# The z projection cut into 16 parts between the attention units, with the tiles around it in another order

## The chip, the core and the metric

The kernel runs on one core of a Trainium2 chip. The metric is the device time of one launch in microseconds (us); lower is better. The core has five engines that run side by side and meet at semaphores: TensorE (PE), VectorE (DVE), ScalarE (ACT), GpSimd (POOL) and SyncE (SP), which issues most of the transfers.

## What is computed

One layer of a hybrid backbone for 128 context tokens and 512 latent tokens (640 in all), width 1024, everything in f32:

```python
x += 0.5*gate1*SwiGLU1(mod(RMSNorm(x)))
h  = mod(RMSNorm(x))
q,k,v (conv, DeltaNet) | z | decay,beta | q_b,k_b,v_b (attention) = h @ w_in
o_a = rmsnorm(delta_forward + delta_backward) * silu(z)      # 8 heads of 64
o_b = rmsnorm(softmax_1 @ v_b - lam * softmax_2 @ v_b)       # 4 heads of 128
x += gate2 * (concat(o_a, o_b) @ w_out)
x += 0.5*gate3*SwiGLU2(mod(RMSNorm(x)))
```

z has 512 columns and is not read before the gate of the DeltaNet output, late in the layer. q_b and k_b also have 512 columns each; they are rotated and then used by the attention.

## The kernel before

Activations lie transposed, features on the partitions and the 640 tokens along the row. A projection goes by **tiles** of 128 output columns: its weights (128x1024) arrive in `w_raw`, ACT rounds them to `w_hi`, DVE makes the rest `w_lo`, and PE runs `dense` (line 1740): for each of 8 blocks of input features and each half of 320 tokens three matmuls (`product`: hi*lo, lo*hi, hi*hi), 48 in all. Two buffers of weights alternate. Every engine's instructions stand in an order written out by hand, and an engine that waits at a semaphore holds up all that stands behind it.

The mixer goes through these stages:

- **Projections.** PE does the 4 z tiles first (ACT applies Silu as it copies them from PSUM into `z_t`), then 12 tiles of q, k and v with the short convolution on DVE, then a loop `for m in range(12, 28)`. It has the last conv tiles (m 12 to 15), q_b (16 to 19), k_b (20 to 23) and v_b (24 to 27, `values`). Within it run a norm of q and k (the helpers of line 2058 and `l2_scale`) and, from m = 20, eight rotations (`rotate`, one a step).
- **Attention units.** `ATT_UNITS` lists 20 units: 4 of the context (128 keys) and 16 of 128 latent queries against 640 keys. In step v PE does `scores(v + 1)` (line 2089, 64 rows deep), `weigh(v - 2)` (line 2110) and `turn(v - 1)` (line 2099, transposes); DVE does the maxima, the combination of the two softmax maps and the copy out; ACT the exponentials and the copy of the turned weights. After every fourth unit comes a **norm** in four steps k (squares on PE, line 2137; root on ACT; spread on PE, line 2123; product on DVE, line 1423), started at v = 6, 10, 14, 18, 22. It has PSUM bank 7, the units' result bank 6. Its result goes to `h_hi[1]`, `h_lo[1]`, which until then hold half of the mixer's input h.
- **Delta tiles**, a list made by `make_schedule` on PE, DVE and POOL, which ends with the first scan step.
- **Scan steps** s = 1 to 4, each with `scan_a`, `scan_b`, `scan_c` on PE for four chains b, and `scan_r`, `scan_u`, `scan_out` on DVE. Between the stages PE does an `attention_part`, 12 matmuls of the attention's half of `w_out`; 16 parts make 8 column blocks m, and DVE adds each to x (`update_attention(m)`).
- **Output.** The DeltaNet output is normed (`o_mean`, `o_norm`), turned (`turn_out`), gated with z (`o_gate`), split (`o_low`, three of five on POOL, line 1726) and multiplied by its half of `w_out`: blocks m = 0 to 3 whole, then `PARTS[2] = [6, 7, 4, 5]` in halves of tokens. The weights of blocks 2i and 2i+1 come as one tile; the last two arrive at places `OUT_POS` 7 and 10 of the ring. FFN 2 follows.

## Time and profile before

| | |
|---|---|
| median of 3 runs | 1712.5 us (1708.83 to 1721.85) |
| the profiled execution | 1717.91 us, span 1715.9 us |
| PE busy | 1642.2 us (96%) |
| weight load busy | 1542.0 us (90%) |
| DVE, ACT, POOL busy | 949.5, 512.2, 208.3 us |
| mean granted clock of TensorE | 0.974 |

The span runs from the first to the last instruction; 2 us of the device time lie around it. Times of places below are us from its start. The clock of TensorE is given as a share of 2.4 GHz; it has two levels, 1.00 and 0.50. A matmul's end is modelled and overlaps the next one's start, so how fast PE really goes is read from the starts. A 32-bit matmul appears as two records, so 4 matmuls of scores are shown as x8.

### The profile page before, as it was taken

Reading aid. Unit: us, or ns where it says so; the run is one execution under the profiler, and the core shown is the slowest. Engines: PE = TensorE matmul, PEld = TensorE weight load, DVE = VectorE, ACT = ScalarE, POOL = GpSimd, SP = SyncE. Lnnn points to the kernel's source line nnn. Section 1 sums busy time; section 2 is a strip of 40 time slices with the busy share of each in tenths; the row PEclk is TensorE's granted clock in tenths of the full one; section 3 lists DMA queues with packets and bytes.
Section 4 is the critical chain, followed back from the end, with each engine's and each line's share of the span. In section 5 each row is a group of like instructions: output and inputs, shape, how many; then the busy total and the mean of one; then the engine's idle time right before and its main releaser. Section 6 shows DMA issues by size and latency. Waiting matters only on the chain.

```text
span 1715.9 us, 27316 instructions
## 1 busy us (share of the span) xinstructions
PE 1642.2 (96%) x10807; PEld 1542.0 (90%) x10807; DVE 949.5 (55%) x1767; ACT 512.2 (30%) x978; POOL 208.3 (12%) x168
## 2 busy tenths in 40 slices
PE   5999999999999999998989999999899999999998
PEld 4899999999999999985778888898899999998886
DVE  5866776666365575436846787676652223321233
ACT  4522222221214434424541111263442222222223
POOL 0000000000000000120015666665000000000000
PEclk9899999999999999996988999998999999999999
DMA  9444444444244122210000000002112222223222
GB/s 279 124 129 147 138 133 136 144 147 147 86 138 132 52 74 73 60 53 13 1 7 1 1 1 1 19 26 74 38 48 75 73 73 73 73 61 98 68 79 87
DMA packets 183811, 136.53 MB, mean 80 GB/s; under 512 B 8192, under 2 KB 169269, under 8 KB 183605
## 3 DMA queue, kind: packets, MB, share of 16 engines
q1 hardware_dynamic: 161029, 112.91, 22.0%
q10 hardware_dynamic: 22704, 22.55, 4.3%
q8 instruction: 53, 0.87, 0.2%
q14 instruction: 25, 0.20, 0.0%
HBM read 132.03 MB, written 3.41 MB: 79 GB/s over the span
## 4 chain that ended last, share of the span: by engine, by line
PE 84%; DVE 9%; issue 2%; ACT 2%; SPq 2%; DMA 1%; POOL 0%; DVEq 0%; ACTq 0%; POOLq 0%
PE ps L1736 19%; PE ps L1737 18%; PE ps L1738 18%; PE ps L2283 3%; PE ps L1883 3%; PE ps L1882 3%; PE ps L1881 3%; PE ps L2287 3%; PE ps L2089 2%; PE ps L1792 1%; PE ps L2211 1%; SPq L434 1%; PE ps L2110 1%; PE ps L2290 1%; PE ps L2263 1%
## 5 line engine op out<-in xcount | busy, mean ns | idle before, releaser
L1736 PE MATMUL ps<-h_hi,w_lo 128*128 128x320 f32 x1760 | 554.2, 315 | 10.8 <-DVE w_lo L1010 4.1
L1737 PE MATMUL ps<-h_lo,w_hi 128*128 128x320 f32 x1760 | 546.9, 311 | 0.0
L1738 PE MATMUL ps<-h_hi,w_hi 128*128 128x320 f32 x1760 | 546.9, 311 | 0.0
L1010 DVE TENSOR_TENSOR w_lo<-w_raw,w_hi 128x1024 fp32r<-128x1024 f32 x158 | 196.0, 1242 | 369.7 <-ACT w_hi L563 368.7
L1736 PEld LDWEIGHTS ps<-h_hi,w_lo 128*128 128x128 f32 x1760 | 333.6, 190 | 15.2 <-DVE h_lo L1056 5.3
L1737 PEld LDWEIGHTS ps<-h_lo,w_hi 128*128 128x128 f32 x1760 | 333.6, 190 | 1.1 <-issue 0.7
L1738 PEld LDWEIGHTS ps<-h_hi,w_hi 128*128 128x128 f32 x1760 | 333.3, 189 | 0.0
L563 ACT CAST w_hi<-w_raw 128x1024 fp32r<-128x1024 f32 x158 | 165.2, 1047 | 215.6 <-PE ps L1738 110.7
L1143 DVE SCALAR_TENSOR_TENSOR ada_acc<-ada_ffn,cond,ada_acc 128x256 f32<-128x256 f32 x336 | 139.0, 479 | 1.1
L657 ACT CAST act_hi<-scratch 128x640 f32 (+1 forms) x44 | 32.0, 728 | 292.1 <-DVE scratch L1183 292.1
L1736 PE MATMUL ps<-act_hi,w_lo 128*128 128x320 f32 (+1 forms) x352 | 109.5, 311 | 0.0
L1738 PE MATMUL ps<-act_hi,w_hi 128*128 128x320 f32 (+1 forms) x352 | 108.7, 309 | 0.0
L1737 PE MATMUL ps<-act_lo,w_hi 128*128 128x320 f32 (+1 forms) x352 | 108.7, 309 | 0.0
L1881 PE MATMUL ps<-w_hi,act_lo 128*128 128x512 f32 x220 | 87.0, 395 | 1.1 <-DVE w_lo L1010 1.1
L1883 PE MATMUL ps<-w_hi,act_hi 128*128 128x512 f32 x220 | 87.5, 398 | 0.0
L1882 PE MATMUL ps<-w_lo,act_hi 128*128 128x512 f32 x220 | 86.9, 395 | 0.0
L1183 DVE TENSOR_TENSOR scratch<-square,ps 128x640 f32<-128x640 f32 x44 | 36.1, 821 | 87.4 <-PE ps L1738 87.4
L650 ACT ACTIVATE square<-ps 128x640 f32<-128x640 f32 x44 | 31.0, 705 | 170.9 <-PE ps L1738 170.6
L1643 POOL MEMSET pre<- 128x24 f32 x3 | 0.2, 121 | 548.7 <-PE ps L1738 548.7
L1737 PEld LDWEIGHTS ps<-act_lo,w_hi 128*128 128x128 f32 x352 | 66.2, 188 | 0.1
L1736 PEld LDWEIGHTS ps<-act_hi,w_lo 128*128 128x128 f32 x352 | 66.2, 188 | 0.1
L1738 PEld LDWEIGHTS ps<-act_hi,w_hi 128*128 128x128 f32 x352 | 66.2, 188 | 0.0
(322 smaller groups left out, 2499.8 us busy)
## 6 DMA issues: line engine op xcount, KB each, us to landing
w_raw<-in_w_ffn_in SPq DMA_DIRECT2D x84, 512.0 KB, 3.8
w_raw<-in_w_ffn_out SPq DMA_DIRECT2D x44, 512.0 KB, 3.8
ada_ffn<-in_w_ada ACTq DMA_DIRECT2D x43, 512.0 KB, 3.6
w_raw<-in_w_in SPq DMA_DIRECT2D x28, 512.0 KB, 3.8
ada_ffn<-in_w_ada SPq DMA_DIRECT2D x13, 512.0 KB, 4.5
ada_tile<-in_w_ada SPq DMA_DIRECT2D x10, 512.0 KB, 8.7
w_raw<-in_w_out SPq DMA_DIRECT2D x8, 512.0 KB, 3.4
ada_wide<-in_w_ada SPq DMA_DIRECT2D x3, 1024.0 KB, 9.7
```

The costliest lines, as they stand in the source:

```text
L563: nc.scalar.copy(w_hi[s if slot is None else slot], w_raw[s][:]).then_inc(w_hi_ready, 1)
L1010: nc.vector.tensor_tensor(w_lo[at], w_raw[s][:], w_hi[at].bitcast(F32), ALU.subtract)\
L1143: ins = nc.vector.scalar_tensor_tensor(a, w, col, a, op0=ALU.mult, op1=ALU.add)
L1183: nc.vector.tensor_tensor(halves(act_f[par][:]), halves(silu_g[par][:]), ps[:, 4 * par + 2:4 * par + 4, 0:HT], ALU.mult).then_inc(act_read ...
L1736: nc.tensor.matmul(out, lo, xh, start=start, stop=False)
L1737: nc.tensor.matmul(out, hi, xl, start=False, stop=False)
L1738: return nc.tensor.matmul(out, hi, xh, start=False, stop=stop)
L1881: nc.tensor.matmul(out, lo, wh, start=first, stop=False)
L1882: nc.tensor.matmul(out, hi, wl, start=False, stop=False)
L1883: ins = nc.tensor.matmul(out, hi, wh, start=False, stop=last)
L2283: four(c, lambda out, h: nc.tensor.matmul(out, m_t[c][:, h, :], t_cols[c][:, h, :], start=True, stop=True))
L2287: four(c, lambda out, h: nc.tensor.matmul(out, x_w[c][:, h, :], tt_cols[c][:, h, :], start=True, stop=True))
```

## The change

- **Projections.** The z tiles no longer come first. The 4 q_b tiles take their place, copied to `q_b`. The loop runs over `m in range(12, 32)`: k_b goes in half tiles (24 matmuls a step, m 16 to 23) and v_b in half tiles (m 24 to 31). The steps of the q and k norm and the rotations keep their numbers m, so they lie closer together.
- **z in the attention.** `z_part(c)`, c = 0 to 15, does 12 matmuls (4 input blocks, one half of the tokens) into bank 6. Steps v = 0 to 2 have two parts, v = 3 to 12 one. Each second part ends a group, and ACT copies it to `z_t` (`z_evict`); the next group waits for that copy. Weights of the z tiles are split in between by ACT and DVE. Silu of z is applied in place later on ACT, between the first `scan_kg` and `scan_first`, with two loads of the activation tables.
- **Norms** start at v = 13, 15, 17, 19, 22 and use bank 6; the units' results go to bank 7.
- **Last scan step.** On PE an attention part stands after each of its stages; before it stood only after the last. On DVE `scan_u` goes ahead of `update_attention(4)` and `o_mean`; `o_norm` of the last three tiles stands ahead of the gates. Three parts are left for the output stage, after `turn_out(2)`, `(3)` and `(4)`; before there were five.
- **w_out.** The tile of blocks 6 and 7 is loaded at place 7 and that of 4 and 5 at place 10; before the two stood the other way round, while the products were done in the order 6, 7, 4, 5.

```diff
@@ -36,7 +36,10 @@
 NU = len(ATT_UNITS)
-NORM_END = NU + 6
+NORM_START = [13, 15, 17, 19, 22]
+NORM_END = NORM_START[-1] + 4
+Z_PARTS = [2, 2, 2, 1, 1, 1, 1, 1, 1, 1, 1, 1, 1]
+Z_DONE = [n for n in range(len(Z_PARTS)) for c in range(sum(Z_PARTS[:n]), sum(Z_PARTS[:n + 1])) if c % 2 == 1]
...
@@ -86,9 +89,9 @@
-def norm_at(v):
-    return divmod(v - 6, 4) if v >= 6 else (None, None)
+def norm_at(v, k):
+    return NORM_START.index(v - k) if v - k in NORM_START else None
...
@@ -122,13 +125,14 @@
 TILE_WIN = FFN_TILES
-TILE_WBV = TILE_WIN + 24
+TILE_WBV = TILE_WIN + 20
+TILE_Z = TILE_WIN + 24
 TILE_WOUT = TILE_WIN + 28
...
 OUT_POS, FFN_EARLY = [0, 1, 2, 3, 4, 5, 7, 10], [6, 8, 9, 11]
-OUT_RING = [0, 1, 2, 3, 4, 5, 6, 7]
+OUT_RING, OUT_COLS = [0, 1, 2, 3, 4, 5, 6, 7], [0, 1, 2, 3, 0, 1, 3, 2]
 TILE_LAST = TILE_FFN[0] + N_IN + 11
@@ -750,7 +757,7 @@
                 act.wait_ge(tile_done, TILE_WIN + i + 1)
-                nc.scalar.activation(halves(z_t[:, i, :]), ps[:, 2 * i:2 * i + 2, 0:HT], ACT.Silu).then_inc(proj_out, 1)
+                nc.scalar.copy(halves(q_b[:, i, :]), ps[:, 2 * i:2 * i + 2, 0:HT]).then_inc(proj_out, 1)
             act.wait_ge(pads_set, 3)
...
@@ -760,11 +767,11 @@
             act.wait_ge(mix_in, 16 * 11)
-            for m in range(12, 28):
+            for m in range(12, 32):
                 if m < 16:
                     to_conv(m - 4, m % 2)
-                elif m < 27:
-                    w_high(TILE_WIN + m + 1, (m + 1) % 2)
+                elif m % 2 == 0:
+                    w_high(TILE_WIN + m // 2 + 9, (m // 2 + 9) % 2)
                 if m < 17:
...
@@ -818,6 +825,11 @@
             ins.then_inc(vb_ready, 1)
+            w_high(TILE_Z + 1, 1)
+            def z_evict(g):
+                act.wait_ge(z_mm, g + 1)
+                nc.scalar.copy(half_of(z_t[:, g // 2, :], g % 2), ps[:, 6, 0:HT]).then_inc(z_out, 1)
...
@@ -851,18 +863,26 @@
                     weights_out(v - 2)
-                j, k = norm_at(v)
-                if k == 0:
+                for g in range(2 * HB):
+                    if Z_DONE[g] == v:
+                        z_evict(g)
+                if v in (2, 5):
+                    i = 2 if v == 2 else 3
+                    w_high(TILE_Z + i, i % 2)
+                j = norm_at(v, 3)
+                if j is not None:
+                    act.wait_ge(an_tmp, j + 1)
+                    nc.scalar.copy(heads4_of(h_hi[1], j), heads4(scratch[0][:, 0:512], P)).then_inc(an_hi, 1)
+                j = norm_at(v, 1)
+                if j is not None:
+                    act.wait_ge(an_mm, j + 1)
+                    nc.scalar.activation(tok_rs[:, 0:4], ps[:, 6, 0:4], ACT.Ln, bias=eps_col[:], scale=D / P).then_inc(an_log, 1)
+                    act.wait_ge(an_log, j + 1)
+                    nc.scalar.activation(tok_rs[:, 0:4], tok_rs[:, 0:4], ACT.Exp, scale=-0.5).then_inc(an_rs, 1)
+                j = norm_at(v, 0)
+                if j is not None:
                     act.wait_ge(s_out, 4 * j + 4)
                     nc.scalar.activation(heads4(square[0][:, 0:512], P), heads4_of(att_q, j), ACT.Square).then_inc(an_sq, 1)
-                if k == 1:
-                    act.wait_ge(an_mm, j + 1)
-                    nc.scalar.activation(tok_rs[:, 0:4], ps[:, 7, 0:4], ACT.Ln, bias=eps_col[:], scale=D / P).then_inc(an_log, 1)
-                    act.wait_ge(an_log, j + 1)
-                    nc.scalar.activation(tok_rs[:, 0:4], tok_rs[:, 0:4], ACT.Exp, scale=-0.5).then_inc(an_rs, 1)
-                if k == 3:
-                    act.wait_ge(an_tmp, j + 1)
-                    nc.scalar.copy(heads4_of(h_hi[1], j), heads4(scratch[0][:, 0:512], P)).then_inc(an_hi, 1)
...
@@ -928,6 +948,9 @@
                 scan_kg(0, b)
+            for i in range(HB):
+                nc.scalar.activation(z_t[:, i, :], z_t[:, i, :], ACT.Silu)
+            load_power_table()
             for b in range(4):
...
@@ -1416,16 +1439,21 @@
                     att_out(v - 2)
-                if k == 2:
+                if v in (3, 6):
+                    i = 2 if v == 3 else 3
+                    w_low(TILE_Z + i, i % 2)
+                j = norm_at(v, 3)
+                if j is not None:
+                    dve.wait_ge(an_hi, j + 1)
+                    nc.vector.tensor_tensor(heads4_of(h_lo[1], j), heads4(scratch[0][:, 0:512], P),
+                                            heads4_of(h_hi[1], j).bitcast(F32), ALU.subtract).then_inc(an_done, 1)
+                j = norm_at(v, 2)
+                if j is not None:
                     dve.wait_ge(an_spread, j + 1)
...
                     nc.vector.scalar_tensor_tensor(heads4(scratch[0][:, 0:512], P), heads4_of(att_q, j), dn_col[:],
-                                                   heads4(ps[:, 7, :], P), op0=ALU.mult, op1=ALU.mult).then_inc(an_tmp, 1)
-                if k == 3:
-                    dve.wait_ge(an_hi, j + 1)
-                    nc.vector.tensor_tensor(heads4_of(h_lo[1], j), heads4(scratch[0][:, 0:512], P),
-                                            heads4_of(h_hi[1], j).bitcast(F32), ALU.subtract).then_inc(an_done, 1)
+                                                   heads4(ps[:, 6, :], P), op0=ALU.mult, op1=ALU.mult).then_inc(an_tmp, 1)
...
@@ -1563,12 +1591,12 @@
                     update_attention(0)
+                for b in range(4):
+                    scan_u(s, b)
                 if s == NT - 1:
...
                         o_mean(p)
-                for b in range(4):
-                    scan_u(s, b)
                 if s == 1:
...
@@ -1586,11 +1614,10 @@
                 o_mean(p)
-            o_norm(2)
+            for p in range(2, NT):
+                o_norm(p)
             o_gate(0)
             o_gate(1)
-            for p in range(OUT_EARLY, NT):
-                o_norm(p)
             update_attention(5)
...
@@ -2033,15 +2061,21 @@
-            for m in range(12, 28):
-                pe.wait_ge(w_lo_ready, TILE_WIN + m + 1)
+            for m in range(12, 32):
+                tile = m if m < 16 else m // 2 + 8
+                pe.wait_ge(w_lo_ready, TILE_WIN + tile + 1)
                 if m < 24:
-                    pe.wait_ge(proj_out, m - 1)
-                    dense(m % 2, 2 * (m % 2)).then_inc(tile_done, 1)
+                    pe.wait_ge(proj_out, tile - 1)
+                    if m < 16:
+                        dense(m % 2, 2 * (m % 2)).then_inc(tile_done, 1)
+                    elif m % 2 == 0:
+                        dense(tile % 2, 2 * (tile % 2), only=0)
+                    else:
+                        dense(tile % 2, 2 * (tile % 2), only=1).then_inc(tile_done, 1)
                 else:
                     if m == 24:
-                        pe.wait_ge(proj_out, 24)
-                    values(m - 24)
+                        pe.wait_ge(proj_out, 20)
+                    values(m // 2 - 12, m % 2)
                 if m == 13:
...
@@ -2107,42 +2141,66 @@
                     vals = cv_tok[:, hb * P:(hb + 1) * P] if nk > P and kt == 0 else v_b[:, kt, hb * P:(hb + 1) * P]
-                    ins = nc.tensor.matmul(ps[:, 6, 0:P], vals, att_wt[:, kt * P:(kt + 1) * P],
+                    ins = nc.tensor.matmul(ps[:, 7, 0:P], vals, att_wt[:, kt * P:(kt + 1) * P],
                                            start=(kt == 0), stop=(kt == nk // P - 1))
...
             pe.wait_ge(vb_ready, 1)
+            def z_part(c):
+                i, half, q = c // 4, c // 2 % 2, c % 2
+                if c % 4 == 0:
+                    pe.wait_ge(w_lo_ready, TILE_Z + i + 1)
+                if c % 2 == 0 and c >= 2:
+                    pe.wait_ge(z_out, c // 2)
+                for k in range(4 * q, 4 * q + 4):
+                    w = (w_hi[i % 2][:, k * P:(k + 1) * P], w_lo[i % 2][:, k * P:(k + 1) * P])
+                    x = [half_of(h[k // 4][:, k % 4, :], half) for h in (h_hi, h_lo)]
+                    ins = product(ps[:, 6, 0:HT], k, w, x, k == 0, k == KD - 1)
+                    if (half, k) == (1, 5):
+                        ins.then_inc(tile_done, 1)
+                if q == 1:
+                    ins.then_inc(z_mm, 1)
             scores(0)
+            z_parts = iter(range(4 * HB))
             for v in range(NORM_END):
-                j, k = norm_at(v)
-                if k == 2:
+                j = norm_at(v, 2)
+                if j is not None:
                     pe.wait_ge(an_rs, j + 1)
                     for i in range(4):
-                        ins = nc.tensor.matmul(ps[:, 7, i * P:(i + 1) * P], tok_rs[:, i:i + 1].broadcast_to([P, P]), ident[:],
+                        ins = nc.tensor.matmul(ps[:, 6, i * P:(i + 1) * P], tok_rs[:, i:i + 1].broadcast_to([P, P]), ident[:],
                                                start=True, stop=True)
                     ins.then_inc(an_spread, 1)
+                if v < len(Z_PARTS):
+                    z_part(next(z_parts))
                 if v + 1 < NU:
...
                     weigh(v - 2)
+                if v < len(Z_PARTS) and Z_PARTS[v] == 2:
+                    z_part(next(z_parts))
                 if 1 <= v <= NU:
                     turn(v - 1)
-                if k == 0:
+                j = norm_at(v, 0)
+                if j is not None:
                     pe.wait_ge(an_sq, j + 1)
...
                     for i in range(4):
-                        ins = nc.tensor.matmul(ps[:, 7, i:i + 1], square[0][:, i * P:(i + 1) * P], ones_d[:, 0:1],
+                        ins = nc.tensor.matmul(ps[:, 6, i:i + 1], square[0][:, i * P:(i + 1) * P], ones_d[:, 0:1],
                                                start=True, stop=True)
...
             for i in range(2 * NT):
+                if i == 2:
+                    pe.wait_ge(an_tmp, 5)
                 if i == 3:
-                    pe.wait_ge(an_tmp, 5)
+                    pe.wait_ge(s_out, NU)
                 if i >= 4:
...
@@ -2295,9 +2353,8 @@
                         stage(s, b)
-                    if (s, stage) != (3, scan_a) and (s < NT - 1 or stage is scan_c):
+                    if (s, stage) != (3, scan_a):
                         attention_part(next(parts))
-            attention_part(next(parts))
...
@@ -2313,13 +2370,12 @@
             turn_out(1)
-            attention_part(next(parts))
             turn_out(2)
-            attention_part(next(parts))
             attention_part(next(parts))
...
             turn_out(4)
+            attention_part(next(parts))
             pe.wait_ge(o_lo, NT)
...
@@ -2328,7 +2384,7 @@
                 for n, m in enumerate(PARTS[2]):
-                    i = 4 + m // 2
+                    i = 9 - m // 2
                     pe.wait_ge(w_lo_ready, TILE_WOUT + OUT_POS[i] + 1)
...
```

How the engines' orders differ at three places. First PE in the steady part of the attention: a step before is scores, weigh (two rows), turn, and then the next scores.

```order
2404 L2089 MATMUL ps<-k_all,q_b 128x320 x4
2405 L2110 MATMUL ps<-att_wt,cv_tok 128x128
2406 L2110 MATMUL ps<-att_wt,v_b 128x128 x4
2407 L2099 MATMUL ps<-ident,sumsq 128x128 x5
2408 L2089 MATMUL ps<-k_all,q_b 128x320 x4
```

The same place on PE in the changed kernel, where lines 1763 to 1765 are `product`.

```order
2349 L1765 MATMUL ps<-h_hi,w_hi 128x320
2350 L2123 MATMUL ps<-k_all,q_b 128x320 x4
2351 L2144 MATMUL ps<-att_wt,cv_tok 128x128
2352 L2144 MATMUL ps<-att_wt,v_b 128x128 x4
2353 L2133 MATMUL ps<-ident,sumsq 128x128 x5
2354 L1763 MATMUL ps<-h_hi,w_lo 128x320
2355 L1764 MATMUL ps<-h_lo,w_hi 128x320
```

Twelve matmuls of a z part now stand between one step's turn and the next step's scores.

Second, PE in the last scan step, before: `scan_a` (2182), `scan_b` (2197) and `scan_c` (2211) one behind the other, then a part.

```order
2830 L2182 MATMUL ps<-st,pre 128x128 x16
2831 L2197 MATMUL ps<-r_s,m_t 128x64 x4
2832 L2197 MATMUL ps<-r_s,x_w 128x64 x4
2833 L2197 MATMUL ps<-r_s,t_cols 128x64 x4
2834 L2197 MATMUL ps<-r_s,tt_cols 128x64 x4
2835 L2211 MATMUL ps<-r_s,m_t 128x64 x4
```

In the changed kernel, PE in the same step (2255 is `scan_b`):

```order
2844 L1765 MATMUL ps<-h_hi,w_hi 128x320
2845 L2255 MATMUL ps<-r_s,m_t 128x64 x4
2846 L2255 MATMUL ps<-r_s,x_w 128x64 x4
2847 L2255 MATMUL ps<-r_s,t_cols 128x64 x4
2848 L2255 MATMUL ps<-r_s,tt_cols 128x64 x4
2849 L1763 MATMUL ps<-h_hi,w_lo 128x320
2850 L1764 MATMUL ps<-h_lo,w_hi 128x320
```

A part of 12 matmuls stands on either side of `scan_b`.

Third, DVE in that step, before: the update of x (three rows), `o_mean`, and only then `scan_u` (1452).

```order
889 L1061 SCALAR_TENSOR_TENSOR x_t<-ps,mods,x_t 128x128
890 L1061 SCALAR_TENSOR_TENSOR x_t<-ps,mods,x_t 128x192
891 L1061 SCALAR_TENSOR_TENSOR x_t<-ps,mods,x_t 128x320
892 L1535 TENSOR_REDUCE o_sum<-t_all 128x8 x3
893 L1452 TENSOR_TENSOR r_s<-ps,beta 128x256 x4
```

DVE there in the changed kernel:

```order
890 L1480 TENSOR_TENSOR r_s<-ps,beta 128x256 x4
891 L1084 SCALAR_TENSOR_TENSOR x_t<-ps,mods,x_t 128x128
892 L1084 SCALAR_TENSOR_TENSOR x_t<-ps,mods,x_t 128x192
893 L1084 SCALAR_TENSOR_TENSOR x_t<-ps,mods,x_t 128x320
894 L1563 TENSOR_REDUCE o_sum<-t_all 128x8 x3
```

`scan_u` now stands ahead of both.

## Rows read from the trace of the kernel before

**Rows 1.** Page, busy time of each engine.

```profile
PE 1642.2 (96%) x10807; PEld 1542.0 (90%) x10807; DVE 949.5 (55%) x1767; ACT 512.2 (30%) x978; POOL 208.3 (12%) x168
```

**Rows 2.** Stretches: length, PE, PEld, DVE, ACT, POOL busy (x), PEclk, DMA share, GB/s.

```profile
732.00:741.00 9.00, 9.00 (x56) 8.20 (x55) 4.36 (x4) 3.10 (x5) 2.15 (x1) 1.00 0.21 58
...
784.00:806.00 22.00, 21.63 (x58) 13.76 (x58) 14.14 (x36) 8.29 (x22) 0.00 (x0) 0.50 0.00 1
806.00:865.00 59.00, 56.84 (x337) 42.34 (x335) 48.84 (x116) 32.88 (x85) 0.00 (x0) 1.00 0.00 1
...
850.00:860.00 10.00, 9.75 (x53) 6.66 (x52) 8.89 (x22) 5.24 (x13) 0.00 (x0) 1.00 0.00 0
```

**Rows 3.** Timeline of PE, first matmuls of two successive tiles (start, us, instruction).

```profile
578.68 0.31 PE L1736 MATMUL ps<-h_hi,w_lo 128*128 128x320 f32 x1
...
585.72 0.31 PE L1736 MATMUL ps<-h_hi,w_lo 128*128 128x320 f32 x1
```

**Rows 4.** Timeline of PE from projection to context units, and ACT's copy between.

```profile
772.27 0.40 PE L2005 MATMUL ps<-w_hi,h_hi 128*128 128x512 f32 x1
...
775.39 0.69 PE L2086 MATMUL ps<-k_b,q_b 64*128 64x128 f32 x4 [1.87 <-ACT v_b L819]
...
772.70 2.54 ACT L819 COPY v_b<-ps 128x512 f32<-128x512 f32 x5 [6.26 <-PE ps L2005]
```

**Rows 5.** Timeline of PE, scores and turn in latent units.

```profile
807.42 1.35 PE L2089 MATMUL ps<-k_all,q_b 64*128 64x320 f32 x8
...
816.61 2.25 PE L2089 MATMUL ps<-k_all,q_b 64*128 64x320 f32 x8
...
820.64 1.34 PE L2089 MATMUL ps<-k_all,q_b 64*128 64x320 f32 x4
...
859.58 2.77 PE L2089 MATMUL ps<-k_all,q_b 64*128 64x320 f32 x8
```

**Rows 6.** Groups of DVE's norm operations in the attention (busy us, mean ns, idle).

```profile
L1423 DVE SCALAR_TENSOR_TENSOR scratch<-q_b,dn_col,ps 128x512 f32<-128x512 f32 x5 | 3.7, 741 | 3.3 <-PE ps L2123 3.3
L1427 DVE TENSOR_TENSOR h_lo<-scratch,h_hi 128x512 fp32r<-128x512 f32 x4 | 2.7, 681 | 0.0
```

**Rows 7.** Timeline of PE, norm steps and the end of the attention.

```profile
849.40 1.06 PE L2123 MATMUL ps<-ident,tok_rs 128*128 128x128 f32 x8
...
864.04 0.95 PE L2137 MATMUL ps<-ones_d,square 128*128 128x1 f32 x8
...
878.62 1.70 PE L2149 MATMUL ps<-ident,pre 128*128 128x128 f32 x7
```

**Rows 8.** Stretches behind the scans, columns as in group 2.

```profile
1175.00:1183.00 8.00, 8.00 (x37) 8.00 (x37) 3.28 (x8) 0.90 (x2) 2.07 (x3) 0.50 0.20 51
...
1199.00:1204.00 5.00, 4.97 (x24) 4.97 (x25) 4.44 (x8) 1.14 (x2) 0.00 (x0) 0.68 0.35 105
...
1220.00:1232.00 12.00, 12.00 (x74) 11.84 (x73) 4.39 (x12) 2.01 (x5) 0.00 (x0) 0.89 0.27 79
```

**Rows 9.** Timeline of ACT around the first scan step, and an earlier table load.

```profile
1061.73 3.92 ACT L897 ACTIVATE square<-k_tok,ekg 128x64 f32<-128x64 f32 x16
1090.29 0.53 ACT L907 COPY st<-ps 64x128 f32<-64x128 f32 x2 [24.64 <-PE ps L2211]
...
681.57 1.28 ACT L773 ACT_TABLE_LOAD   x1
```

**Rows 10.** Timeline of PE and POOL, last scan step to the output's matmuls.

```profile
1174.65 1.76 PE L2211 MATMUL ps<-r_s,m_t 128*128 128x64 f32 x8 [1.13 <-DVE r_s L1452]
...
1181.29 0.61 PE L1736 MATMUL ps<-h_hi,w_lo 128*128 128x320 f32 x1
...
1199.03 0.64 PE L1736 MATMUL ps<-h_hi,w_lo 128*128 128x320 f32 x1 [2.22 <-DVE h_lo L1556]
...
1188.76 3.37 POOL L1726 TENSOR_TENSOR h_lo<-scratch,h_hi 128x512 fp32r<-128x512 f32 x2 [11.69 <-ACT h_hi L966]
```

**Rows 11.** Waits of PE from 1210 to 1222 (total, times, longest).

```profile
PE ps L1736 <- DVE w_lo L1010: 3.3, 1, 3.3
```

44 lines of the change are left out of this document (24 added, 20 removed).

## Prediction

> **What bounds the kernel now.** I read the page first, then PE in stretches, then the timelines at the places that the change touches. PE is busy 96% of the span [rows 1], so a gain must come from PE's idle time or from time in which it is slow; the change takes no matmul away. A busy share hides both. In the attention PE shows 56.84 of 59 us busy at a clock of 1.00, and 21.63 of 22 us at 0.50 [rows 2]. The reader should see two things. First, from 784 to 806 every matmul takes twice its time. Second, at full clock eleven steps (807.42 to 859.58) take 52.2 us, 4.74 each with their norms, while one step in which PE never waited took 4.03 (816.61 to 820.64, its scores 2.25 instead of 2.77) [rows 5]. In a stretch of two steps without norms DVE is busy 8.89 of 10 us [rows 2], 4.1 us of a 4.6 us step. DVE and the chain through it set the pace there, and PE has about 0.6 us of slack a step. Elsewhere PE waits and is slow at three places behind the scans [rows 8, 10, 11].
>
> The Trainium skill (Trainium Kernel Development and Optimization, "Performance Expectations") says that a matmul's busy time is a bad measure and that the busy share of weight loads is a good one. By the former the attention has 2 us of room, by the latter (42.34 of 59 us, rows 2) some 17 us; the starts bear out the latter.
>
> **1. The projections lose four tiles.** A tile of 48 matmuls takes 7.04 us (578.68 to 585.72) [rows 3], 1.76 per 12. Four tiles: -28.2 us. k_b and v_b in half tiles cost PE nothing, since its weight loads are per matmul anyway. What runs beside them gets closer: a step of the loop has 3.5 us of projection instead of 7.0. A step with norm and rotation took 9 us with DVE busy 4.36, ACT 3.10 and POOL 2.15 [rows 2]; it becomes 5.4 us long (9 less half a tile of 3.5), which still covers each of them, and w_hi and w_lo are made in every second step only. So I take 0 (bounds 0 and +2, for waits in the chain of that norm). The copy of v_b that PE waits for stays: 2.54 us, with scores starting 3.1 us after the last values matmul started [rows 4].
>
> **2. The attention takes the z parts.** Before, from the first scores at 775.39 to the turns of k at 878.62: 103.2 us [rows 4, 7]. After, at full clock:
> - Steps 0 to 2: six parts, 10.6 us; the small context matmuls, some 0.7 a step, 2.1; three waits for the eviction of bank 6. A copy of 512 columns takes 0.5 us (a fifth of 2.54 [rows 4]), with the signals 0.6 each, 1.8. Together 14.5.
> - Steps 3 to 5: three parts 5.3, three scores of 2.2, the rest 1.6: 13.5.
> - Steps 6 to 12: a full step and a part, 4.03 + 1.76 = 5.79 on PE against DVE's 4.1. Seven: 40.5. PE becomes the bound, and DVE's chain has 1.7 us more to answer in.
> - Steps 13 to 18: no z, but a norm every second step. On PE 0.9 for squares and 1.0 for the spread [rows 7] make 5.0 a step; on DVE 0.74 + 0.68 [rows 6] make 4.8. The squares of norm j now wait for the product of norm j-1 in the same step, and DVE does that product behind the copy of the weighed unit: about 0.3 a step more. Six times 5.1 to 5.3: 31.
> - Steps 19 to 25: before, 864.95 (end of the squares) to 878.62, 13.7 us; one norm more falls into it: 15.
>
> Sum 114.5, against 103.2: +11.3 for 28.2 us of work, net -16.9. To this comes the clock. The 3.1 us without matmuls before the first scores will bring it to 0.50, as it did at 776. The question is how long. Before, it stayed at 0.50 until 806 under scores 64 rows deep, PE busy all the time [rows 2]. With dense projection matmuls it came back in 3 to 5 us: from 1199 the mean is 0.68 over 5 us of them, so some 3.2 us were slow, and from 1220 it is 0.89 over 12 us, 2.6 us slow [rows 8]. After the change dense parts follow at once, so I take 4 us at half speed, +2 (bounds 0 and the rival below). For signals between a part and its neighbours 0.15 to 0.2 in some 13 steps, +2.5. **Net -12.4** (bounds -17 and -3).
>
> **3. Silu of z** goes to ACT behind `scan_kg`, where ACT is idle 24.64 us [rows 9]: four Silus of 640 columns at some 0.75 and two loads at 1.28 [rows 9] make 5.6. Cost 0; without that cover it would be on the scan's chain. The Trainium skill (ScalarE: Activation LUTs, "What ACT_TABLE_LOAD costs") puts a switch at about 2.66 us with its drain. By that it would be 8.3 us, still hidden; no row here shows the drain.
>
> **4. The last scan step.** DVE's update and `o_mean` make PE wait 1.13 us before `scan_c`, after which the clock is 0.50 from 1175 to 1183 [rows 8, 10]. `scan_c` takes 6.6 us there (1174.65 to 1181.29) against 3.5 at full clock. After, `scan_b` ends with `scan_u` right behind it and a part on PE in between: no wait, and no fall of the clock. Before, PE had done a and b when it began to wait, at 1173.5 (1174.65 less 1.13). Two parts of 1.8 now lie among them, so `scan_c` starts at 1177.1 and ends at 1180.6 instead of 1181.3. Behind it stands one part instead of two, and at full speed: the first turn comes at 1182.4 instead of some 1186. From the first turn: two gates 1.4 and the norms before them bring the first split to 1187.4, against 1188.7 before; POOL then has three, at 1.7 each (3.37 for two) to 2.2 when DVE runs beside it [rows 10]: 1192.5 to 1194. The update of block 5, on which a part waits, adds idle PE time, not length. The output's matmuls start at 1194.2 instead of 1199.03, **-4.8** (bounds -8 and -1). PE will idle longer here than before, so the low clock at their start stays.
>
> **5. The w_out tiles.** PE waits 3.3 us for the last tile's `w_lo` [rows 11]. After, blocks 6 and 7 (3.5 us of halves) come first, and the late tile is needed 3.5 us later, when it is just ready. The stretch after the wait has a mean clock of 0.89 over 12 us [rows 8], 1.3 us lost, which goes too. **-4.5** (bounds -5 and -1, if the new order of blocks waits for an update of x instead).
>
> Delta tiles and scans 1 to 3 do the same as before: 0.
>
> **Sum**: -12.4 - 4.8 - 4.5 = -21.7. The profiled execution took 1717.9 us, so 1696.2 by itself; it lies 5.4 above the median of 1712.5, and the forecast for the median is **1691 us**.
>
> **The rivals.**
> - *The attention is bound by latency, not by PE.* Then a z part adds to a step of 4.6 instead of filling its slack: 6.4 for seven steps (+4), 5.7 for the six with norms (+2.5), and one us more in the last ones. For it: the maxima wait for scores and scores for exponentials in turn, and a part stands ahead of the scores. Against: the one unhindered step, and that the exponentials of the step before can run under the part. Total -14: **1698**. The same time comes out if terms 4 and 5 only move their waits on.
> - *The low clock lasts (slower).* The place is the start of the attention. If the scores' 64 rows keep the clock at 0.50 as they did for 30 us before, the z parts pay double too: 28 us of full-speed work in steps 0 to 5 take 56, +28 instead of +2. That turns the gain into +4, and each further step costs 5.8: with the first two heavy steps, **1728**. It decides when the slow stretch holds more than 24 us of full-speed work. Before, that stretch had long runs of scores alone; now at most 2.2 us stand between two parts. That speaks against it.
> - *The clock is back at once and the output's chain shrinks by the full 8 us.* Then -12.4 becomes -15, term 4 -7.5, and the sum is -27: **1685**.
>
> **How the numbers follow.** Forecast (1686 to 1696) 0.5; latency or moved waits 0.27; better case 0.15; slow clock 0.06; nothing of it works 0.02. The range of 8 in 10 takes in the first three but for their outer ends: 1681 to 1703. A measurement of this kernel tells a difference of about 1%, 17 us, from none. Below 1695.4 lie most of the forecast's own range and the better case: faster 0.61. Slower by 1% needs the slow clock: 0.05. Same 0.34.
>
> **What would show it.** In the profile after: first scores near 747 to 748; the granted clock back at 1.00 by some 753; steps 6 to 12 at 5.8 to 6.0 us; turns of k near 866; no wait of `scan_c` for `r_s` and a clock of 1.00 there; the output's matmuls 4 to 5 us closer to the end of the scan; no wait for `w_lo` behind block 3. The prediction is wrong if steps with z take 6.4 us or more, if the clock is 0.50 past step 3, or if the projections gain less than 27 us because the norm of q and k or a rotation holds PE up.

## Result and the profile after

| | before | changed |
|---|---|---|
| median | 1714.61 us (1708.83 to 1721.85, 4 runs) | 1691.34 us (1687.52 to 1693.84, 4 runs) |
| ratio, 95% interval | | 0.9851, [0.981, 0.9892] |
| profiled execution, span | 1717.91, 1715.9 us | 1687.52, 1685.7 us |
| mean granted clock | 0.974 | 0.991 |

The change takes 1.5% away; by the interval it is 1.1 to 1.9%, all of it beyond the 1% that the prediction took for the least that can be told. The two profiled executions lie 30.4 us apart and the medians 23.3: the one of before is 3.3 above its median, the other 3.8 below. So a difference between the two traces, taken stage by stage, overstates the gain by some 7 us in all.

The page of the changed kernel:

```profile
PE 1612.6 (96%) x10807; PEld 1518.5 (90%) x10807; DVE 945.2 (56%) x1767; ACT 518.0 (31%) x988; POOL 207.1 (12%) x168
```

Against [rows 1] the number of PE's records is the same and the busy share is the same 96%. That line alone says nothing of where 30 us went. The starts of five instructions do. Each is read from the timeline of its own kernel; e1, e2, e3 and r1 are runs told of below, r1 a second run of the changed kernel.

| start, us | before | changed | e1 | e2 | e3 | r1 |
|---|---|---|---|---|---|---|
| first scores | 775.39 | 748.40 | 775.41 | 774.15 | 747.97 | 748.84 |
| turns of k | 878.62 | 865.78 | 877.86 | 887.88 | 865.41 | 871.39 |
| last `scan_a` | 1166.27 | 1149.00 | 1160.30 | 1171.22 | 1148.52 | 1153.82 |
| output's matmuls | 1199.03 | 1175.75 | 1191.38 | 1197.99 | 1176.48 | 1180.57 |
| FFN 2 | 1235.41 | 1205.67 | 1222.83 | 1232.93 | 1211.45 | 1210.47 |
| span | 1715.9 | 1685.7 | 1703.8 | 1713.2 | 1692.0 | 1693.4 |

From before to changed: projections -27.0, attention +14.1 (103.2 to 117.4), turns of k to the last `scan_a` -4.4, to the output's matmuls -6.0, to FFN 2 -6.5, the rest -0.4: -30.2.

The attention of before is not one number, though. e1 and e2 have the same instructions there as before, and it took 103.2 us in before, 102.5 in e1 and 113.7 in e2; the changed kernel's took 117.4, 117.4 (e3) and 122.6 us (r1). The +14.1 is one pair out of these; the means of three and three differ by 12.7. The clock goes with it. The attention of before, changed and e2 as stretches (columns as in [rows 2]; each line is of the kernel whose starts it has):

```profile
775.39:878.62 103.23, 94.53 (x476) 69.48 (x477) 72.61 (x188) 49.15 (x135) 0.00 (x0) 0.83 0.02 6
748.40:865.78 117.38, 106.33 (x668) 86.76 (x669) 75.83 (x191) 54.63 (x146) 0.00 (x0) 0.97 0.06 19
774.15:887.88 113.73, 99.85 (x477) 75.24 (x478) 72.85 (x188) 49.57 (x135) 0.00 (x0) 0.77 0.02 5
```

**The attention.** Timeline of PE in the changed kernel: the first scores, three steps with a z part, and steps with a norm (lines 1763 to 1765 are `product`, 2123 scores, 2144 weigh, 2133 turn, 2193 squares, 2207 turns of k). A part's first matmul is shown; its other eleven are in the dots:

```profile
748.40 0.49 PE L2120 MATMUL ps<-k_b,q_b 64*128 64x128 f32 x4 [2.73 <-ACT v_b L826]
...
801.92 2.01 PE L2123 MATMUL ps<-k_all,q_b 64*128 64x320 f32 x8
...
805.54 0.39 PE L1763 MATMUL ps<-h_hi,w_lo 128*128 128x320 f32 x1
...
807.48 1.84 PE L2123 MATMUL ps<-k_all,q_b 64*128 64x320 f32 x8
809.25 0.49 PE L2144 MATMUL ps<-att_wt,cv_tok 128*128 128x128 f32 x2
809.57 1.06 PE L2144 MATMUL ps<-att_wt,v_b 128*128 128x128 f32 x8
810.47 0.71 PE L2133 MATMUL ps<-ident,sumsq 128*128 128x128 f32 x5
810.93 0.39 PE L1763 MATMUL ps<-h_hi,w_lo 128*128 128x320 f32 x1
...
812.87 2.01 PE L2123 MATMUL ps<-k_all,q_b 64*128 64x320 f32 x8
...
822.85 1.35 PE L2123 MATMUL ps<-k_all,q_b 64*128 64x320 f32 x8
...
832.97 1.02 PE L2193 MATMUL ps<-ones_d,square 128*128 128x1 f32 x8 [0.86 <-DVE scratch L1455]
...
844.43 1.02 PE L2193 MATMUL ps<-ones_d,square 128*128 128x1 f32 x8 [1.24 <-DVE scratch L1455]
...
865.78 6.62 PE L2207 MATMUL ps<-ident,pre 128*128 128x128 f32 x40
```

The reader should compare the scores. Between 801.92 and 812.87 steps follow each other by 5.56 and 5.39 us; the six from the scores at 780.01 to those at 812.87 take 32.9, 5.48 each, where 5.79 was forecast. The eight records span 2.01 and 1.84 us there, but 1.35 at 822.85, as at 807.42 in [rows 5]. So a step's own work on PE is 1.94 (the part, 805.54 to 807.48) + 1.29 (from the scores at 822.85 to the weigh behind them) + 1.22 + 0.46 (809.25 to 809.57 to 810.47 to 810.93) = 4.91, and 0.57 of the 5.48 is still a wait of scores, inside a group that shows no wait: at 801.92 the second map's first matmul starts 0.67 us after the first map's, at 822.85 it starts 0.01 after.

The waits of PE from 745 to 870 (total, times, longest):

```profile
PE ps L2120 <- ACT v_b L826: 2.7, 1, 2.7
PE ps L2193 <- DVE scratch L1455: 2.7, 3, 1.2
PE ps L2123 <- ACT exps L858: 2.3, 3, 0.9
PE ps L2193 <- ACT square L885: 2.2, 1, 2.2
...
PE ps L1763 <- ACT z_t L832: 1.4, 3, 0.5
```

The second line is new: squares of one norm wait for the product of the norm before. Stretches of the changed kernel (columns as in [rows 2]):

```profile
748.00:760.00 12.00, 10.58 (x70) 9.36 (x71) 5.27 (x21) 4.42 (x17) 0.00 (x0) 1.00 0.16 45
775.00:822.00 47.00, 46.02 (x285) 37.02 (x283) 34.90 (x84) 24.05 (x60) 0.00 (x0) 1.00 0.08 23
822.00:852.00 30.00, 25.61 (x165) 20.02 (x163) 21.23 (x50) 16.07 (x43) 0.00 (x0) 0.94 0.00 1
878.00:920.00 42.00, 34.34 (x249) 30.30 (x248) 26.60 (x54) 7.16 (x23) 27.11 (x22) 0.92 0.00 1
1149.00:1176.00 27.00, 24.32 (x191) 23.60 (x190) 21.88 (x41) 14.02 (x39) 14.04 (x12) 1.00 0.22 63
```

In 775:822 PE is busy 98% at a clock of 1.00; in 822:852, where z is done and the norms stand, 85% at 0.94. The last line is the last scan step, at full clock throughout; before it had 0.50 from 1175 to 1183 [rows 8]. 878:920 is the start of the delta tiles, whose instructions are the same in both kernels, and still the clock differs there, since the same stretch before shows 0.72:

```profile
878.00:920.00 42.00, 35.25 (x201) 31.01 (x199) 18.40 (x44) 13.84 (x37) 17.29 (x14) 0.72 0.03 7
```

**Silu.** Timeline of ACT in the changed kernel:

```profile
1044.47 3.92 ACT L917 ACTIVATE square<-k_tok,ekg 128x64 f32<-128x64 f32 x16
1048.40 1.28 ACT L952 ACT_TABLE_LOAD   x1
1049.70 2.62 ACT L952 ACTIVATE z_t<-z_t 128x640 f32<-128x640 f32 x4
1052.32 1.28 ACT L599 ACT_TABLE_LOAD   x1
...
1073.03 0.53 ACT L927 COPY st<-ps 64x128 f32<-64x128 f32 x2 [19.42 <-PE ps L2269]
```

It takes 5.2 us (1048.40 to 1053.60), and ACT then waits 19.42 us for PE: hidden, as forecast.

**The output.** Timeline of PE in the changed kernel:

```profile
1175.75 0.42 PE L1763 MATMUL ps<-h_hi,w_lo 128*128 128x320 f32 x1 [1.05 <-DVE h_lo L1584]
```

Neither `scan_c`'s wait for `r_s` nor the 3.3 us for `w_lo` is there any more. PE waits 1.05 us before the output's matmuls where it waited 2.22 [rows 10]; "PE will idle longer here than before" was wrong. The clock behind this wait, in the changed kernel and then in e3, which waits 2.22 us there:

```profile
1175.00:1180.00 5.00, 4.25 (x29) 4.25 (x30) 4.83 (x10) 1.79 (x2) 0.00 (x0) 1.00 0.34 111
1176.00:1181.00 5.00, 4.52 (x20) 4.52 (x21) 4.75 (x9) 1.60 (x2) 0.00 (x0) 0.66 0.33 105
```

All three profiles with the wait of 2.2 us have the low clock behind it (0.68 in before, 0.66 in e1 and e3), none of the eleven with 1.05 to 1.08 us has it.

### The profile page after: what moved, and what is told of

The parts are those of the page before. It is cut to its first block, busy times and chain, and to the rows that moved or that the text cites. A ratio compares the mean times of both kernels' runs of the same rounds, so it can differ in the third digit from the quotient of the medians.

```text
span 1685.7 us, 27313 instructions
## 1 busy us (share of the span) xinstructions
PE 1612.6 (96%) x10807; PEld 1518.5 (90%) x10807; DVE 945.2 (56%) x1767; ACT 518.0 (31%) x988; POOL 207.1 (12%) x168
## 4 chain that ended last, share of the span: by engine, by line
PE 85%; DVE 9%; ACT 2%; SPq 2%; issue 2%; DMA 1%; POOL 0%; DVEq 0%; ACTq 0%; POOLq 0%
PE ps L1763 19%; PE ps L1765 19%; PE ps L1764 19%; PE ps L2341 3%; PE ps L1910 3%; PE ps L1909 3%; PE ps L1908 3%; PE ps L2345 3%; PE ps L1819 1%; PE ps L2123 1%; PE ps L2255 1%; PE ps L2269 1%; SPq L439 1%; PE ps L2348 1%; PE ps L2144 1%
```

## Experiments

The kernel before ran beside each; ratios are against it, with the 95% interval. A ratio is not always the quotient of the two medians (for e1 that is 0.9939), and medians of runs that were not measured together are compared with care: before has 1714.6, 1721.7, 1717.6 and 1716.8 us beside changed, e1 to e4, e5 to e8, and the rest. Four groups: parts of the change alone, the amount and place of z's work, the two waits that the change made, and repeats.

**e1_tiles_only**: the kernel before with the order of the last two w_out tiles alone.

```diff
-OUT_RING = [0, 1, 2, 3, 4, 5, 6, 7]
+OUT_RING, OUT_COLS = [0, 1, 2, 3, 4, 5, 6, 7], [0, 1, 2, 3, 0, 1, 3, 2]
...
-                    i = 4 + m // 2
+                    i = 9 - m // 2
```

Expected:

> The kernel before with one change: the weight tile of output blocks 6 and 7 arrives at place 7 of the ring and that of 4 and 5 at place 10. My account (term 5): the 3.3 us wait of PE for w_lo goes, and with it the low clock behind it, 4 to 6 us less than before (ratio 0.997). Rival, that the wait only moves to an update of x or to the late tile: within 1 us of before.

Measured: 1711.16 us (1704.82 to 1717.37), ratio 0.9964 [0.9938, 0.9991]. The wait for `w_lo` is gone. From the output's matmuls to FFN 2 it takes 31.45 us instead of 36.38, -4.9. The medians differ by more (1721.7 of before in these runs), but the interval holds -1.5 to -10.7 us and so says no more than the trace does. This is what was expected, and not the rival's 1 us.

**e2_scan_only**: the kernel before with the last scan step and the output stage reordered, as in the changed kernel.

```diff
+                for b in range(4):
+                    scan_u(s, b)
                 if s == NT - 1:
                     update_attention(4)
                     for p in range(OUT_EARLY):
                         o_mean(p)
-                for b in range(4):
-                    scan_u(s, b)
...
-                    if (s, stage) != (3, scan_a) and (s < NT - 1 or stage is scan_c):
+                    if (s, stage) != (3, scan_a):
```

Expected:

> The kernel before with the last scan step and the output stage of the changed one: scan_u ahead of the update of x and of the sums, a part after each stage on PE, norms ahead of the gates. My account (term 4): no wait before scan_c, no fall of the clock there, the output's matmuls 5 to 6 us closer to the start of the step; 5 to 6 us less. Rival, that the late tile of weights then holds PE up longer, since the ring did not get faster: only 1 to 3 us less, and the wait for w_lo grows from 3.3 us.

Measured: 1715.4 us (1705.24 to 1717.09), ratio 0.9959 [0.9935, 0.9984]. Last `scan_a` to the output's matmuls: 26.77 us instead of 32.76, 6.0 closer, where 5 to 6 were expected. The wait for `w_lo` stays at 3.3 us and doesn't grow, against the rival. The stretch of it, in e2:

```profile
1171.00:1198.00 27.00, 24.30 (x192) 23.57 (x190) 21.77 (x40) 13.81 (x39) 14.28 (x12) 1.00 0.24 67
```

The clock stays at 1.00. The waits of PE from 1150 to 1222 in e2 begin with the one that this part doesn't touch:

```profile
PE ps L1735 <- DVE w_lo L1010: 3.3, 1, 3.3
PE ps L1735 <- DVE h_lo L1556: 1.1, 1, 1.1
```

**e3_z_only**: the changed kernel with both of these as before.

```diff
-                    i = 9 - m // 2
+                    i = 4 + m // 2
...
-                for b in range(4):
-                    scan_u(s, b)
                 if s == NT - 1:
                     update_attention(4)
                     for p in range(OUT_EARLY):
                         o_mean(p)
+                for b in range(4):
+                    scan_u(s, b)
```

Expected:

> The changed kernel with the last scan step, the output stage and the w_out tiles as before, so the z parts, the half tiles and the late norms alone. My account: 12 to 13 us less than before up to the turns of k, and the same gain at the end, ratio 0.9925. Rival, that the gain of the z parts is lost again behind them: under 8 us. If the delta tiles gain 4 us more, as in the profile of the changed kernel, that is the clock and not the change, and the ratio comes out between 0.990 and 0.993.

Measured: 1697.72 us (1693.78 to 1705.93), ratio 0.988 [0.9844, 0.9916]. The waits of PE from 1150 to 1222 in e3:

```profile
PE ps L1764 <- DVE w_lo L1033: 3.3, 1, 3.3
PE ps L1764 <- DVE h_lo L1584: 2.2, 1, 2.2
...
PE ps L2270 <- DVE r_s L1480: 1.1, 1, 1.1
```

The old waits are back, `w_lo`, `h_lo` (L1584) and `r_s` alike. Yet last `scan_a` to the output's matmuls takes 27.96 us here and not 32.76: after the same 1.1 us of waiting the clock did not fall this time (1.00 over 1148 to 1177, where e1 has 0.89 over 1160 to 1192). With the old order the stretch takes 32.76 (before), 31.08 (e1) and 27.96 us (e3); with the new one it takes 26.75 to 26.77 in all eleven profiles that have it (e2, changed, e4 to e9, r1 to r3). So the reorder itself is worth 27.96 - 26.75 = 1.2, and beside that it takes away a loss to the clock that was 3.1 and 4.8 us in two profiles of three and none in the third. z alone gives 1.2% (0.8 to 1.6%, 14 to 27 us), and the 0.9925 that was expected lies outside the interval: the z parts bring more than the account had for them. e1 and e2 give 0.4% each by their ratios, too little to be told apart by times. The three ratios add up to 2.0% against the 1.5% of the whole, which their intervals allow.

**e4_third_z**: the changed kernel with 4 of the 12 matmuls of each part.

```diff
-                    ins = product(ps[:, 6, 0:HT], k, w, x, k == 0, k == KD - 1)
+                    ins = nc.tensor.matmul(ps[:, 6, 0:HT], w[0], x[0], start=(k == 0), stop=(k == KD - 1))
```

Expected:

> The changed kernel with only the hi*hi product in the z parts, so 4 of 12 matmuls each; z then lacks its two correction products. 128 matmuls of 0.147 us, 18.8 us, leave PE. If PE bounds the steps with z, they shrink by nearly all of it, 14 to 18 us in the attention. If the parts lie in slack of the chain of maxima and exponentials, steps 6 to 12 cannot go below 4.6 us: they lose 0.8 of 1.18 us each, and the whole attention 9 to 12 us.

Measured: 1689.05 us (1685.33 to 1696.26), ratio 0.9813 [0.977, 0.9857]; 2 us below the changed kernel by the medians, 0.4% by the ratios, whose intervals overlap, for 18.8 us of matmuls less (two thirds of 28.2). Its profiled execution is the longest of the four, and its attention takes 125.6 us, more than the 117.4 with all of z. Both expectations missed. Stretches of e4:

```profile
748.00:760.00 12.00, 9.95 (x40) 7.49 (x41) 5.69 (x24) 4.86 (x18) 0.00 (x0) 0.63 0.17 45
767.00:850.00 83.00, 74.14 (x350) 57.03 (x348) 52.90 (x125) 37.52 (x94) 0.00 (x0) 0.77 0.06 20
```

And its waits of PE from 749 to 875:

```profile
PE ps L2123 <- ACT exps L858: 6.1, 7, 1.4
PE ps L2193 <- DVE scratch L1455: 5.3, 3, 2.7
```

The changed kernel has a clock of 0.98 in 767:850 and the kernel before 0.81. With a third of z the scores wait seven times for exponentials, and the clock averages 0.77. So it can't say what a step would take at full clock with less work. What it points to is another use of the parts: with them whole, PE stays at its higher level. The stretches are of one profile, but the mean clock of whole executions agrees: 0.977 to 0.984 in the four of e4, 0.987 to 0.991 in the four of the changed kernel.

**e5_late_parts**: no part in steps 0 to 2, two each in steps 3 to 8.

```diff
-Z_PARTS = [2, 2, 2, 1, 1, 1, 1, 1, 1, 1, 1, 1, 1]
+Z_PARTS = [0, 0, 0, 2, 2, 2, 2, 2, 2, 1, 1, 1, 1]
...
```

Expected:

> The changed kernel with no z part in steps 0 to 2 and two in each of steps 3 to 8 (weight splits moved along). My account: the dense parts in the context steps fill waits and keep the clock up. Without them PE waits 2 to 4 us in steps 0 to 2 and the clock falls to 0.50 there until the parts of step 3, so 4 to 8 us more than the changed kernel. Rival, that the context steps' waits cost nothing because the same matmuls only move: within 1.5 us.

Measured: 1696.39 us (1691.33 to 1698.87), ratio 0.9871 [0.9839, 0.9903]; attention 121.7 us. The context units wait for exponentials three times, 2.4 us in all, and the clock from 748 to 760 is 0.57:

```profile
748.00:760.00 12.00, 9.56 (x35) 7.54 (x36) 7.14 (x30) 4.18 (x19) 0.00 (x0) 0.57 0.18 46
```

A mean of 0.57 of two levels puts (1 - 0.57) / 0.5 = 86% of the 12 us at half speed. Behind them, under parts two a step, it is 1.00 (767 to 850). It comes back in the first part of step 3, of which the first and the last matmul in e5 are:

```profile
755.69 0.61 PE L1763 MATMUL ps<-h_hi,w_lo 128*128 128x320 f32 x1
...
758.77 0.45 PE L1765 MATMUL ps<-h_hi,w_hi 128*128 128x320 f32 x1
```

Its matmuls stand 0.27 us apart, at half speed, and those of the next part 0.15. So the low clock lasted 10 us here and 24 to 31 with the order of before (before, e1, e2), which has no dense matmuls at this place. The time itself tells little: the attention is 4.3 us longer than the changed kernel's 117.4, as expected, but shorter than the 122.6 that the same changed kernel took in r1.

**e6_product_first**: on DVE the norm's product goes to the head of its step, ahead of the maxima.

```diff
             for v in range(NORM_END):
+                j = norm_at(v, 2)
+                if j is not None:
+                    dve.wait_ge(an_spread, j + 1)
...
                 if v + 1 < NU:
                     att_max(v + 1, 0)
```

Expected:

> The changed kernel with the product of a norm at the head of DVE's step instead of its end. The squares then do not wait for it: PE's three waits for that product, 2.7 us in sum, go, and the fall of the clock at 846 with them: 2.5 to 5 us less than the changed kernel in the attention. Rival, that the steps with norms are bound by DVE's sum of work (4.8 us a step), so that the wait moves to the scores: under 1 us.

Measured: 1687.31 us (1683.56 to 1691.86), ratio 0.9828 [0.9797, 0.9859]. The wait of the squares is gone; in e6 they follow the turn at once:

```profile
830.86 0.71 PE L2133 MATMUL ps<-ident,sumsq 128*128 128x128 f32 x5
831.40 0.95 PE L2193 MATMUL ps<-ones_d,square 128*128 128x1 f32 x8
832.28 1.90 PE L2123 MATMUL ps<-k_all,q_b 64*128 64x320 f32 x8
```

Its attention takes 113.0 us against 117.4, both with a clock of 1.00 in 748:760: -4.3, within the 2.5 to 5 that were expected. Of it 2.7 are the waits for the product; squares also wait 1.0 us for ACT instead of 2.2, and scores 1.6 for exponentials instead of 2.3. The clock hardly has a part in it: at half speed are 6.0 us of the changed kernel's attention and 5.4 of this one's, 0.3 us of loss apart, and the fall at 846 that was to go is there in e6 at 845.

**e8_part_ahead**: the first z part goes ahead of PE's wait for `v_b`.

```diff
-            pe.wait_ge(vb_ready, 1)
...
+            z_part(next(z_parts))
+            pe.wait_ge(vb_ready, 1)
             scores(0)
```

Expected:

> The changed kernel with z part 0 ahead of the first scores, in the 2.7 us in which PE waits for the copy of v_b. Part of 1.76 us moves into the wait: 1.5 to 1.8 us less than the changed kernel. Rival, that the context steps are a chain through the evictions, in which the part was hidden already: under 0.5 us.

Measured: 1690.54 us (1685.73 to 1693.55), ratio 0.9843 [0.9813, 0.9874]. PE's wait there falls from 2.73 to 0.88 us, and the attention, from first scores to turns of k, from 117.4 to 116.8. The turns of k come 1.5 us earlier (864.31), but 0.9 of this is there at the first scores already (747.52 instead of 748.40), and without this edit they start anywhere from 747.53 to 748.84. So 0.6 us is what the trace gives to the edit, less than the 1.5 to 1.8 expected: the part went into the gap, and a new wait of 1.1 us for the exponentials stands behind the first scores. The median moves by less than can be told.

**e7_both**: e6 and e8 together.

```diff
+            z_part(next(z_parts))
+            pe.wait_ge(vb_ready, 1)
             scores(0)
...
+                j = norm_at(v, 2)
+                if j is not None:
+                    dve.wait_ge(an_spread, j + 1)
```

Expected:

> The changed kernel with both edits, the norm's product at the head of DVE's step and z part 0 ahead of the first scores. The gains are at different places and should add: 4 to 6.5 us less than the changed kernel. If either is hidden, the sum of what the two single runs show.

Measured: 1685.88 us (1683.78 to 1690.21), ratio 0.9809 [0.9779, 0.9839]. Beside it e6 has 1687.31 us, so what e8's edit adds can't be told here either. Against the changed kernel's 1691.34 it is 5.5 us less, as expected, but the two weren't measured together.

**Repeats**, measured together on one chip: the changed kernel, e7 and e6 again.

Expected:

> The changed kernel once more, on the chip of the next three. Ratio to before 0.985 as in its first four runs, 0.981 to 0.989. Its profile tells how far the low clock moves between runs of one kernel: the step from the turns of k to the second scan step took 231.7 us after 236.1 before with the same instructions, which I put down to 6.8 against 20.5 us at half clock there.

> The changed kernel with the norm's product at the head of DVE's step and z part 0 ahead of the first scores, beside the changed kernel on the same chip: 4 to 6 us less if the single runs add (4.3 us in the attention of the first, 0.6 of the second in the profiles); within 2 us of it if the clock eats it.

> The changed kernel with only the norm's product at the head of DVE's step, beside the changed kernel on the same chip: 3 to 5 us less, and again no wait of the squares for the product.

Measured, six runs each: r1 1692.1 us (1688.7 to 1695.17), 0.9846 [0.9811, 0.9882]; r2 1684.99 us (1684.45 to 1698.7), 0.9828 [0.9787, 0.987]; r3 1685.73 us (1681.73 to 1689.17), 0.9809 [0.9773, 0.9844]. The product first is 6.4 us better than the change as it is (3 to 5 were expected), the second time that it comes out lower; both together are 7.1 better (4 to 6), so the part ahead adds nothing that can be told. The clock of r1 at the start of the attention:

```profile
748.00:760.00 12.00, 10.64 (x53) 9.32 (x54) 4.21 (x17) 3.57 (x12) 0.00 (x0) 0.72 0.16 45
```

It is the same kernel with the same wait for `v_b`, and here 0.72 instead of 1.00: 56% of 12 us at half speed, 3.4 us lost, in an attention of 122.6 us.

**e9_part_between**: in steps 6 to 12 the z part stands between the scores of the two softmax maps.

```diff
                 for m in range(2):
+                    if m == 1 and between is not None:
+                        between()
```

Expected:

> The changed kernel with the z part of steps 6 to 12 between the scores of the two maps instead of ahead of both. The trace shows 8 records of scores in 1.35 us where nothing waits and 4 in 1.34 us where the second map waits, so the matmuls of the two maps, on rows 0 to 63 and 64 to 127, seem to run side by side. If so, the part parts them and a step costs some 0.5 to 1.0 us more, 4 to 7 us over the seven. Rival, that the second map's wait for its exponentials is what makes the scores long: the part then fills that wait, and the steps get shorter, by up to 0.3 us each.

Measured: 1702.49 us (1698.06 to 1707.02), ratio 0.9916 [0.9882, 0.9949]: 10.4 us more than r1 by the medians; its attention takes 129.3 us against r1's 122.6, both with a clock of 0.72 in 748:760. These 6.7 us are within the 4 to 7 expected and are what the traces place; the other 3.7 of the medians they do not. Timeline of PE in e9:

```profile
790.78 1.34 PE L2125 MATMUL ps<-k_all,q_b 64*128 64x320 f32 x4
792.05 0.49 PE L2146 MATMUL ps<-att_wt,cv_tok 128*128 128x128 f32 x2
792.38 1.06 PE L2146 MATMUL ps<-att_wt,v_b 128*128 128x128 f32 x8
793.27 0.71 PE L2135 MATMUL ps<-ident,sumsq 128*128 128x128 f32 x5
793.91 1.34 PE L2125 MATMUL ps<-k_all,q_b 64*128 64x320 f32 x4
795.18 0.41 PE L1763 MATMUL ps<-h_hi,w_lo 128*128 128x320 f32 x1
```

None of these scores waits, and one map alone (x4) takes 1.34 us: as long as both together where nothing parts them (x8, 1.35 at 822.85 of the changed kernel, where their starts are 0.01 us apart). The two maps have their 64 rows of keys in the two halves of the array, and issued in turn they run side by side. Parted, a step takes 6.35 us (787.56 to 793.91 between first scores), 0.87 more than 5.48; seven such steps make 6.1 of the 6.7 us. The rival, that the part would fill a wait of the second map and shorten the steps, is refuted. By the sum 4.91 + 1.29 = 6.20, so here PE's own work does set the step. The Trainium skill (TensorE: Matmul & The Clock Gate, "Why this matters for your kernels") says that matmuls of small K in different row groups can run at the same time; this trace agrees.

## Why the prediction was right, and where it was not

The forecast of 1691 us met the measured 1691.34. Some of that is luck: the sum of -21.7 stands against -23.3 between the medians and -30.2 between the two traces, and errors of both signs lie in it.

What the prediction has no term for is how much of the gain goes with the clock. The mean granted clock was 0.968 to 0.981 in the 46 executions of the kernel before that ran beside the experiments, and 0.986 to 0.991 in all ten of the changed kernel (r1 included). Span times clock, the length of a run counted at full speed, is 1671.3 us (1715.9 x 0.974) before and 1670.5 (1685.7 x 0.991) after, and over all executions the medians of this product differ by 3 us. So nearly all that the change saves was time at half speed, and mostly through the z parts: e1 and e2 alone stay at 0.974 to 0.982, e3 has 0.982 to 0.990. This doesn't make the slack a mistake, as a slow PE also fills it: the three steps of before from 788.50 to 807.42 took 18.9 us at a mean clock of 0.53, where three steps at full speed take 13.8 (3 x 4.6). It says that the parts have two uses, to fill the waits and, by filling them, to end the stretches at half speed. How the gain divides between the two, no run here shows.

1. **Projections**, -28.2: -27.0, within its bounds. Of the 1.2 missing, 0.9 is a longer wait for `v_b` (2.73 instead of 1.87 us). The first scores themselves move by 1.3 us between executions (774.15 to 775.41 in before's order, 747.5 to 748.8 in the new one).
2. **Attention**, net -12.4: from 103.2 to 117.4 us, where 103.2 + 15.8 = 119.0 was forecast; with the projections' 27.0 that is net -12.8. That parts would take far less time than the 28.2 us of their work was right. That the size came out so close is luck in part: it was taken against 103.2, which is 113.7 in e2 with the same instructions, and e3, the z parts alone, gives more by its ratio (20.7 us, 14 to 27) than these -12.4. Inside it:
   - Steps 6 to 12 were put at 5.79 and took 5.48 (5.51 with the edges: 38.6 us for the seven, where 40.5 was forecast). What failed is the reading "one step in which PE never waited took 4.03". Its scores took 2.25 us against 1.35 in the same rows [rows 5]: that was a wait inside the group. PE's slack of a step before was 4.6 - (1.29 + 1.22 + 0.46) = 1.6 us and not 0.6. The 17 us of 59 that the prediction read from the weight loads are 1.4 a step of 4.74, close to that; the forecast did not use them.
   - Steps 13 to 18 were put at 31 and took 33.4. "About 0.3 a step more" for the squares' wait was right in kind (2.7 us in three waits); exponentials and a lower clock (0.94) came on top. e6 takes this wait away, with 4.3 us.
   - Steps 0 to 2 took 15.5 (14.5), steps 3 to 5 14.2 (13.5), steps 19 to 25 15.7 (15).
   - The clock, "4 us at half speed, +2": 0 in the changed kernel's profile, 3.4 in r1, 5.2 in e7's profile (0.57 over 12 us). Put at 2 us of cost, it lies in the middle of what happens from run to run.
3. **Silu**, 0: shown hidden, 5.2 us against 5.6. The table loads take 1.28 us, and the operation behind starts 1.30 after the load. The drain that the Trainium skill puts into a switch (ScalarE: Activation LUTs, "What ACT_TABLE_LOAD costs", about 2.66 us) does not show here.
4. **Last scan step**, -4.8: -6.0 between the traces, -1.2 with no loss to the clock on either side (e3 against changed), and 1.5 more behind it, in the stretch of term 5. Its point "no wait, and no fall of the clock" is shown in eleven profiles. That the fall it removes is there in every execution of before was taken from one trace, and is not so. "The low clock at their start stays" was wrong too: PE waits 1.05 us there instead of 2.22, and 1175:1180 is at 1.00.
5. **w_out tiles**, -4.5: -6.5 between the traces, -4.9 in e1 (31.45 against 36.38 us). The stretch from the output's matmuls to FFN 2 takes 36.38 us in before, 34.94 in e2, 34.97 in e3, 31.45 in e1 and 29.92 in changed. This fits three pieces: the wait with its edges, 3.5 (tiles); the low clock behind the wait for `h_lo`, 1.5 (which the scan's order takes away: before, e1 and e3 have it); the low clock behind the wait for `w_lo`, 1.5 (before and e2 have it, e3 does not: 1.00 over 1195 to 1212). So of the 6.5 the tiles have 5.0 and the scan's order 1.5, and changed against e3 is the wait and the first low clock.
6. **Delta tiles and scans**, 0: -4.4 between the traces, with the same instructions. The clock of 878:920 was 0.72 in before's profile and 0.92 in the changed kernel's. It differs as much among kernels whose instructions there are the same: 0.92 in r1 and r2 but 0.76 in r3 and 0.78 in e7. The whole stretch, from the turns of k to the last `scan_a`, took 282.4 to 283.5 us in ten of the fourteen profiles, e1 and e2 with before's order among them, and 286.5 to 287.7 in four (before, e5, e7, r3). So it is a matter of the execution and not of the change.

**The rivals.** *Bound by latency*: its price of 6.4 us a step is wrong, but steps 6 to 12 still hold 0.57 us of waiting, and only with more PE work (e9) 0.15; neither it nor the forecast is the whole. e4, made to settle this, could not, and what a step would take at full clock with less of z stays open. *The low clock lasts*: it did not in any of the ten further profiles with z parts; from 767 on the clock is 0.94 to 1.00, e4 with its third of z excepted, where 0.77 bears out what this rival feared, under another load. *The better case* of 1685 is below the changed kernel and was come near only with the product first (e6 1687.3, e7 1685.9, r2 1685.0, r3 1685.7).

## What to carry to other kernels

Work moved into an engine's idle time should be priced by what the engine's own instructions take when nothing waits, read from the shortest group of the same kind, and not from a step that shows no wait: a group's span can hold one. Where a part of the change adds a wait of its own (squares for the product), look at once whether one instruction of the other engine can stand earlier; here that gave 6.4 us by medians measured together, beside the change's 23.3. Before two traces are subtracted, compare the stretches that the change doesn't touch: 4.4 us of 30.2 lay there, and the attention of before differed by 11 us between executions of the same instructions. And multiply the span by the mean granted clock on both sides: here that product hardly moved, which tells that the gain was time at half speed.
